# A pre-norm's squares summed in column groups beside a fourth output, and root's table loaded ahead of the post-norms

## The reference

```python
def rms_norm(x, g):
    y = x * lax.rsqrt(jnp.mean(x * x, axis=-1, keepdims=True) + 1e-6)
    return y * g

def squared_relu_mlp(h, w1, w2):            # w1 1024x4096, w2 4096x1024
    return jnp.square(jax.nn.relu(h @ w1)) @ w2

for layer in range(2):
    hn = rms_norm(h, mix_pre_g[layer])
    m = conformer_conv(hn, ...) if layer == 0 else mla_attention(hn, ...)
    h = h + rms_norm(m, mix_post_g[layer])
    f = squared_relu_mlp(rms_norm(h, ffn_pre_g[layer]), w_ff1[layer], w_ff2[layer])
    h = h + rms_norm(f, ffn_post_g[layer])
```

## Time and profile before

| | |
|---|---|
| median of 3 runs | 1212.76 us (1208.52 to 1216.09) |
| profiled execution | 1209.91 us, its span 1208.1 us |
| TensorE busy | 1160.0 us, 96% of the span |
| weight loads of TensorE (beside matmuls) | 993.7 us, 82% |
| VectorE, ScalarE, GpSimd busy | 848.7, 669.8, 213.5 us |
| mean granted clock of TensorE | 0.989 of full |
| HBM read | 205.09 MB, 172 GB/s |

### The profile page before, as it was taken

One profiled execution on the slowest core, in us unless ns is written; L12 is line 12 of the kernel. 1 busy time (PEld: TensorE's weight loads), 2 busy tenths in 40 slices (PEclk: granted clock), 3 DMA queues, 4 the chain that ended last, 5 costly groups with the idle time before them and its releaser, 6 DMA issues.

```text
span 1208.1 us, 26351 instructions
## 1 busy us (share of the span) xinstructions
PE 1160.0 (96%) x10538; PEld 993.7 (82%) x10538; DVE 848.7 (70%) x1390; ACT 669.8 (55%) x1024; POOL 213.5 (18%) x166
## 2 busy tenths in 40 slices
PE   8999999999899999999999999999999999999997
PEld 6888888888666888888877678888887777888886
DVE  5656876655864886555677468888777665888775
ACT  5435566433656566433565566665556656666542
POOL 0000000000002000000032433554231333355400
PEclk8999999999999999999999999999999999999999
DMA  7871355555251355555232334554465334455452
GB/s 292 275 243 65 118 222 208 209 207 195 86 209 71 139 209 210 209 189 190 108 106 106 139 140 156 217 215 152 175 242 196 109 116 179 162 209 211 142 196 78
DMA packets 22250, 208.37 MB, mean 172 GB/s; under 512 B 2464, under 2 KB 8992, under 8 KB 9120
## 3 DMA queue, kind: packets, MB, share of 16 engines
q1 hardware_dynamic: 22176, 207.32, 47.4%
HBM read 205.09 MB, written 2.23 MB: 172 GB/s over the span
## 4 chain that ended last, share of the span: by engine, by line
PE 54%; issue 17%; DVE 12%; POOL 6%; ACT 6%; DMA 4%; SPq 0%; POOLq 0%; DVEq 0%; ACTq 0%
PE ps L654 13%; PE ps L656 13%; PE ps L655 13%; POOL tmp L1941 5%; DVE w_lo L2013 4%; DMA staged<-weights 3%; ACT w_hi L1384 2%; POOL probs L1950 1%; PE ps L812 1%; PE ps L665 1%; PE ps L667 1%; PE ps L835 1%; PE ps L666 1%; PE ps L710 1%; PE ps L787 1%
## 5 line engine op out<-in xcount | busy, mean ns | idle before, releaser
L1384 ACT ACTIVATE w_hi<-staged 128x2048 f16<-128x2048 f32 (+1 forms) x192 | 356.2, 1870 | 196.9 <-PE ps L656 156.1
L2013 DVE SCALAR_TENSOR_TENSOR w_lo<-staged,w_hi 128x2048 f16<-128x2048 f32 (+1 forms) x192 | 429.3, 2249 | 44.1 <-ACT w_hi L1384 43.9
L654 PE MATMUL ps<-f_hi,w_hi 128*128 128x256 f16 x1596 | 435.1, 273 | 4.4 <-DVE w_lo L2013 2.1
L656 PE MATMUL ps<-f_hi,w_lo 128*128 128x256 f16 x1596 | 435.0, 273 | 0.0
L655 PE MATMUL ps<-f_lo,w_hi 128*128 128x256 f16 x1596 | 435.0, 273 | 0.0
L654 PE MATMUL ps<-x_hi,w_hi 128*128 128x256 f16 x928 | 253.8, 274 | 5.8 <-DVE x_lo L2043 2.9
L655 PE MATMUL ps<-x_lo,w_hi 128*128 128x256 f16 x928 | 253.4, 273 | 0.0
L656 PE MATMUL ps<-x_hi,w_lo 128*128 128x256 f16 x928 | 253.4, 273 | 0.0
L654 PEld LDWEIGHTS ps<-f_hi,w_hi 128*128 128x128 f16 x1596 | 156.1, 98 | 25.1 <-issue 3.4
L655 PEld LDWEIGHTS ps<-f_lo,w_hi 128*128 128x128 f16 x1596 | 156.2, 98 | 18.3
L656 PEld LDWEIGHTS ps<-f_hi,w_lo 128*128 128x128 f16 x1596 | 156.2, 98 | 18.1
(11 more groups left out here) (304 smaller groups left out, 1588.9 us busy)
## 6 DMA issues: line engine op xcount, KB each, us to landing
staged<-weights SPq DMA_DIRECT2D x82, 2048.0 KB, 8.1
staged<-weights SPq DMA_DIRECT2D x16, 1408.0 KB, 6.2
qT<-u_rows SPq DMA_DIRECT2D x16, 143.0 KB, 3.2
kT<-u_rows SPq DMA_DIRECT2D x16, 143.0 KB, 3.7
staged<-weights SPq DMA_DIRECT2D x2, 1024.0 KB, 8.3
u_rows<-probs SPq DMA_DIRECT2D x8, 144.0 KB, 4.6
cst<-constants SPq DMA_DIRECT2D x1, 1031.5 KB, 16.2
h<-x_turned SPq DMA_DIRECT2D x1, 1024.0 KB, 5.2
```

The costliest lines, as they stand in the source:

```text
L654: pe.matmul(out, wh, xh[:, c, :], start=(c == 0), stop=False)
L656: last = pe.matmul(out, wl, xh[:, c, :], start=False, stop=(c == kc - 1))
L1384: act.activation(w_hi[:, s, o:o + n], staged[:, s, o:o + n], ACT.Copy, scale=SW).then_inc(hi_split, 1)
L2013: dve.scalar_tensor_tensor(w_lo[:, s, o:o + n], staged[:, s, o:o + n], SW, w_hi[:, s, o:o + n], ALU.mult, ALU.subtract).then_inc(lo_split, 1)
```

## The change

Layers 0 and 1, norms `ffn_pre_0` and `ffn_pre_1` only (the loop ahead of the kv product keeps its three outputs and its own sums):

- The arrival loop has four outputs (`RING`) for three. It doesn't add a square per chunk. At chunk 5 and behind the loop `group_sums` sums four squares at once: four matmuls with a 32-column matrix of ones, each into its own 32 partitions of bank 7 (column groups), the second set accumulating on the first.
- ScalarE copies that bank to SBUF (`group_copied`); in output 4, ahead of chunk 4, TensorE sums the copy per token (each sum stands 32 times there, which the root's scale divides out); root and reciprocal run on 128x2; in output 5, ahead of chunk 1, TensorE spreads the scale; VectorE copies it to `LATE_SCALE` (`copy_late`), and only then drains.
- Outputs 4 and 5 of the first round go to banks 4 and 5 (`hidden_bank`), so they wait for no drain. Output 6 goes to bank 2 and waits for the third drain, output 7 to bank 3 and for the fourth.
- `root_next` is called ahead of the layer norm's squares, ahead of `square_last` of mix_post_0, behind the sines in `mlp(0)`, and ahead of the `wo` product's splits.

```diff
@@ -224,8 +224,14 @@
 ADDED = (*POSTS, "final")
 ADDED_AT = {_name: (DC - 1) * _i for _i, _name in enumerate(ADDED)}
 
-BY_TOKEN = ("mix_pre_0", "layer_norm", "mix_post_0", "ffn_post_0", "mix_post_1", "ffn_post_1", "attn_0",
+BY_TOKEN = ("mix_pre_0", "layer_norm", "mix_post_0", "ffn_pre_0", "ffn_post_0", "mix_post_1", "ffn_pre_1", "ffn_post_1", "attn_0",
             "g_ckv", "attn_1", "final")
+
+GROUPED = ("ffn_pre_0", "ffn_pre_1")
+GROUPS = 4
+
+
+LATE_COPIED = ("ffn_pre_0", "ffn_pre_1", "attn_0")
 
 SUM_BANK = {"layer_norm": 4, "attn_0": 4}
 COLUMN = {"g_ckv": 4}
...
@@ -550,6 +558,11 @@
         def even_bank(n):
 
             return n if n < 3 else (n - 3) % 2
+
+        def hidden_bank(i, n):
+
+
+            return n if isinstance(i, int) and i == 0 and n < RING + 2 else n % RING
 
         def wait_from(engine, semaphore, value):
 
@@ -734,6 +747,11 @@
                         return
                     pe.matmul(STAT, k("ones"), stat[:, 4, :], start=True, stop=True).then_inc(summed, 1)
                     return
+                if name in GROUPED:
+
+                    pe.wait_ge(group_copied, GROUPED.index(name) + 1)
+                    by_token(6, stat[:, 0, :], True, True).then_inc(summed, 1)
+                    return
                 if name in ADDED_AT:
 
                     pe.wait_ge(m_added, ADDED_AT[name] + n - 1)
@@ -764,6 +782,27 @@
                     last = pe.matmul(STAT, k("ones"), sq[:, c, :], start=(c == 0), stop=(c == DC - 1))
                 if c == DC - 1:
                     last.then_inc(summed, 1)
+
+            def group_sums(name, first):
+
+
+                if first == 0:
+                    pe.wait_ge(rooted, NORM_AT[name])
+                pe.wait_ge(squared, SQUARE_AT[name] + first + GROUPS)
+                n = P // GROUPS
+                for r in range(GROUPS):
+                    last = pe.matmul(ps[n * r:n * r + n, 7, 0:T], k("ones")[:, 0:n], sq[:, first + r, :], start=(first == 0),
+                                     stop=(first + GROUPS == DC))
+                if first + GROUPS == DC:
+                    last.then_inc(group_summed, 1)
+
+            def grouped(name):
+
+                def fresh(c):
+                    if c == GROUPS + 1:
+                        group_sums(name, 0)
+                    pe.wait_ge(x_lo_ready, SPLIT_AT[name] + c + 1)
+                return fresh
 
             def begun(name):
 
@@ -929,19 +968,30 @@
                 one, two = f"ff1_{layer}", f"ff2_{layer}"
                 u0 = FIRST[one]
 
-                def hidden_chunk(i, n):
+                def hidden_chunk(i, n, fresh=None):
 
                     s, j = n // 4, n % 4
                     if j % 2 == 0:
                         pe.wait_ge(lo_split, i * 4 + (2 * (u0 + s) + j // 2 + 1))
 
-                    wait_from(pe, drained[one], i * 8 + (n + 1 - RING))
-                    features(ps[:, n % RING, 0:T], (u0 + s) % 2, j * DC * P, DC, x_hi, x_lo).then_inc(product[one], 1)
-
-                together(one, 3, x_hi, x_lo, begun(f"ffn_pre_{layer}"))
-                add_square(f"ffn_pre_{layer}", DC - 1)
-                for n in range(3, 8):
-                    hidden_chunk(0, n)
+                    b = hidden_bank(i, n)
+                    if b < RING:
+                        wait_from(pe, drained[one], i * 8 + (n + 1 - RING))
+                    features(ps[:, b, 0:T], (u0 + s) % 2, j * DC * P, DC, x_hi, x_lo, fresh).then_inc(product[one], 1)
+
+                def norm_sums(n):
+
+                    def fresh(c):
+                        if (n, c) == (4, 4):
+                            sums(f"ffn_pre_{layer}")
+                        if (n, c) == (5, 1):
+                            spread_scale(f"ffn_pre_{layer}", inverted, NORM_AT[f"ffn_pre_{layer}"] + 1)
+                    return fresh
+
+                together(one, RING, x_hi, x_lo, grouped(f"ffn_pre_{layer}"))
+                group_sums(f"ffn_pre_{layer}", GROUPS)
+                for n in range(RING, 8):
+                    hidden_chunk(0, n, norm_sums(n))
                 with pe.Fori(1, dict(STREAM)[one] // 2) as i:
                     for n in range(8):
                         hidden_chunk(i, n)
@@ -1158,7 +1208,7 @@
                         dot(2 * n - 10)
                         dot(2 * n - 9)
                     if n == 6 and c == 1:
-                        pe.wait_ge(late_ready, 1)
+                        pe.wait_ge(late_ready, LATE_COPIED.index("attn_0") + 1)
                         sums("g_ckv")
                     if n == 7 and c == 1:
                         spread_scale("g_ckv", inverted, NORM_AT["g_ckv"] + 1)
@@ -1418,8 +1468,9 @@
                     dst, src = root_col[:, o:o + TT], ps[:, b:b + TT, 0]
                 else:
                     dst, src = stat[:, 0, :], STAT
+                copies = P // GROUPS if name in GROUPED else 1
                 act.activation(dst, src, ACT.Sqrt, bias=k("input_eps" if late else "rms_eps"),
-                               scale=(INV ** -2 if late else 1.0) / (P * NORM_CHUNKS[name])).then_inc(rooted, 1)
+                               scale=(INV ** -2 if late else 1.0) / (P * NORM_CHUNKS[name] * copies)).then_inc(rooted, 1)
 
             def square_last(name, norm, bank, scale, bias=0.0):
 
@@ -1540,6 +1591,7 @@
                     conv_out(j - CONV_LAG - 1)
             for c in range(DC - CONV_LAG - 1, DC):
                 conv_out(c)
+            root_next()
             for c in range(DC):
                 act.wait_ge(ln_centred, c + 1)
                 act.activation(sq[:, c, :], conv[:, c, :], ACT.Square).then_inc(ln_squared, 1)
@@ -1563,6 +1616,8 @@
                 one, two = f"ff1_{layer}", f"ff2_{layer}"
                 for c in range(DC):
                     begin(f"ffn_pre_{layer}", x_hi, h_ready[f"mix_{layer}"], 0, c)
+                act.wait_ge(group_summed, layer + 1)
+                act.activation(stat[:, 0, :], STAT, ACT.Copy).then_inc(group_copied, 1)
                 root(f"ffn_pre_{layer}")
                 u0 = FIRST[one]
 
@@ -2055,6 +2112,10 @@
                     return SPREAD_SCALE
                 dve.wait_ge(inverted, NORM_AT[name] + 1)
                 return stat[:, 1, :]
+
+            def copy_late(name):
+
+                dve.tensor_copy(LATE_SCALE, scale_there(name)).then_inc(late_ready, 1)
 
             def scale(name, src, gain, dst, lag=1, meanwhile=None):
 
@@ -2290,7 +2351,8 @@
 
                 split(2 * u0 + 2)
                 invert(f"ffn_pre_{layer}")
-                dve.wait_ge(inverted, NORM_AT[f"ffn_pre_{layer}"] + 1)
+                copy_late(f"ffn_pre_{layer}")
+                dve.wait_ge(late_ready, LATE_COPIED.index(f"ffn_pre_{layer}") + 1)
 
                 def hidden_low(i, n):
 
@@ -2305,7 +2367,7 @@
                     dve.wait_ge(product[one], i * 8 + (n + 1))
 
                     wait_from(dve, f_hi_ready[layer], i * 8 + (n - 1))
-                    dve.scalar_tensor_tensor(tmp[:, n % 2, :], ps[:, n % RING, 0:T], 0.0, LATE_SCALE, ALU.max,
+                    dve.scalar_tensor_tensor(tmp[:, n % 2, :], ps[:, hidden_bank(i, n), 0:T], 0.0, LATE_SCALE, ALU.max,
                                              ALU.mult).then_inc(drained[one], 1)
                     if n or not isinstance(i, int):
                         hidden_low(i, n - 1)
@@ -2500,7 +2562,7 @@
                 for i in E_SWAP.get(n, ()):
                     rope("even", i)
                 if n == 3:
-                    dve.tensor_copy(LATE_SCALE, SPREAD_SCALE).then_inc(late_ready, 1)
+                    copy_late("attn_0")
                 if n == 6:
                     forget_first()
                     weigh(0)
```

More of the change, by code:

```diff
@@ L417, in conformer_mla_fox_dsa_moba_kernel @@
         late_ready = sem("late_ready")
+        group_summed = sem("group_summed")
+        group_copied = sem("group_copied")
         part_product = sem("part_product")
@@ L1969, in decays @@
                         [P, T]), ALU.mult).then_inc(decay_rows, 1)
-            pool.wait_ge(late_ready, 1)
+            pool.wait_ge(late_ready, LATE_COPIED.index("attn_0") + 1)
             for n in (4, 5, 6, 7):
```

## The result

| | before | changed |
|---|---|---|
| median | 1209.82 us (19 runs, 1205.38 to 1216.15) | 1214.96 us (19 runs, 1208.98 to 1219.09) |
| ratio | | 1.0036, 95% interval 1.0021 to 1.0051 |
| span of the profiled execution | 1208.1 us | 1212.7 us |
| mean granted clock | 0.989 | 0.986 |

The ratio is estimated from all the runs of both kernels and is not that of the two medians, which differ by 5.1 us. By it the changed kernel is slower by 4.4 us (2.5 to 6.2), well inside the 1% that was called "same". The forecast of 1214.7 us looks closer than it is: it stood on the median 1212.76 of three runs, and 19 runs put before at 1209.82. What was forecast is a difference of +1.9 us; what was measured is +4.4. One execution of the kernel before in the experiments took 2407 us and is left out throughout.

The account below looks back on a forecast made before the run. It took TensorE, busy nearly the whole span, as the bound, so edits act only at the seams. Tables -1.1, loops +1.8 and clock +1.2 gave +1.9 us on the median 1212.76: 1214.7 us, range 1208 to 1219.

Parts of the forecast that it names:

- The table: Post-norms: early loads of root's table let the root start sooner, by 0.55, 0.62 and 0.08 us; counted as -1.1 us.
- The term of mix_post_0: Post-norm mix_post_0: root 0.55 us sooner, of which some 0.40 is left because more warm-up matmuls run at half clock.
- The rival by which the switch frees more than the load: Three post-norms: the table switch holds ScalarE up a load's length more, so 3 x 1.28 us more gained, 1210.9; chance 0.05.
- The four column groups: Arrival loops of layers 0 and 1: a set of four grouped square sums takes 0.68 us, bounds 0.44 and 1.74.
- The series rival: Arrival loops: the four groups run one after another, 1.74 us for 0.68 a set, +4.2 us, 1218.9; chance 0.12.
- their cover: Outputs 4 and 5: ScalarE's copy has 1.31 us, root and small reciprocal 2.01 us, before TensorE needs their results.
- The drain: Behind each loop: first drain 2.46 us later, TensorE waits 2.13 at output 6; output 7 +0.9 us, twice +1.8.
- The clock: Behind the output 6 waits: TensorE drops to half clock after one of two, +1.2 us, bounds 0 and +2.4.
- the drains don't bind: First hidden product, layers 0 and 1: only TensorE's own account counts, 1.71 us ahead per layer, -4.5, 1208.2; chance 0.12.

Follow-up runs that it names:

- tables_only: The kernel before with the four early table loads alone; ratio 0.9991 (0.9969 to 1.0014) to the kernel before.
- free_drains: The changed kernel with two half-unit weight splits moved out of the way of VectorE's drains; ratio 0.9977 (0.9952 to 1.0003) to the kernel before.
- early_spread: The changed kernel with per-token sum and spread moved forward to chunks 2 and 6 of output 4; ratio 1.0010 (0.9990 to 1.0030) to the kernel before.
- after_again: The changed kernel a second time, with no edit; ratio 1.0046 (1.0022 to 1.0069) to the kernel before.
- loop_only: The changed kernel without the four early table loads; ratio 1.0050 (1.0029 to 1.0071) to the kernel before.
- both_early: The changed kernel with both the splits of free_drains and the positions of early_spread; ratio 0.9965 (0.9944 to 0.9986) to the kernel before.

## Why the prediction was right or wrong

The direction, the class and the mechanism held; the difference was put too small, by two terms that were mis-sized: the table edit's in mix_post_0 and, above all, the clock's. That the total came within 0.3 us of the measured median is luck: the median it was added to stood 2.9 too high, the difference 2.5 too low.

- **The table.** Gains of 0.57, 0.61, 0.10 for 0.55, 0.62, 0.08, and none in the layer norm, whose root still waited 1.51 us for TensorE after the early load. The term of mix_post_0 was mis-sized: I let the half clock in its warm-up stay and took 0.40; it went, and layer 0's stretch shows 1.39. The rival by which the switch frees more than the load has no row for it: root 0.62 after the sum, as in the post-norm that never had a load.
- **The four column groups.** 136.60 - 135.83 = 0.77, less 0.11 for the fp16 matmul, is 0.66 us a set, for 0.68 taken from two groups of 64 columns. The series rival (1.74) is out. ScalarE's copy, the per-token sum and the spread fell inside their cover, as said.
- **The drain.** First drain 4.42 behind the loop's end for 4.45; wait at output 6 2.14 for 2.13; at output 7 0.38 for 0.47. I had TensorE start the loop late; here the chunk's arrival started it (0.54 idle at 129.12), since the warm-up ran at full clock, with no effect on what follows the loop. One loop costs 1.04 us (177.45 less 176.41 of tables_only) for the 0.9 forecast. free_drains shows that it is the queue behind the drain, early_spread that the drain's own start counts one for one.
- **The clock**, the term that failed in size. I counted one stretch behind two waits, at 1.2. In three profiles (changed, after_again, loop_only) five of the six waits of 2.14 us have half clock behind them. At the price of 1.28 that is 1.28 x 5 / 3 = 2.1 us a run, for 1.2. The fourteen seams of the other seven profiles, where the wait is 1.15 us or less or is filled, have none.
- **The sum again with measured terms**: tables -1.39 - 0.61 - 0.10 = -2.1, loops 2 x 1.04 = +2.1, clock +2.1: +2.1 us, just below the measured 2.5 to 6.2. About half of what lies above is clock too, by the clock on record with every run: 0.9851 on average over the changed kernel's 29 runs, 0.9878 over 69 runs of the kernel before. That is 36.1 and 29.4 us at half clock, 6.7 more (3.8 to 9.5). A us at half clock costs 0.38 us, by the slope of time against it within each kernel (182 runs), the same as 1.28 for a stretch of 3.41. By an estimate from these figures the clock's share of the difference is 2.5 us. The sum above holds 1.3 of it: 2.1, less the 0.8 by which the 1.39 of mix_post_0 exceeds its 0.57. With 1.2 more it comes to 3.3, inside the interval. In which places this further half clock lies is open. A candidate is mix_post_1's warm-up, 0.7 to 1.1 us of time where it comes: 6 of 10 profiles have it, with and without either edit, and I can't tie it to one. The other half clocks ahead of the seams (3.41, 6.83 or 10.24 us in the layer norm) change from one execution to the next as well.
- **The rival "the drains don't bind"**, 1208.2, was no outcome of this change, but its price was right: both_early builds it and stands 4.2 below before, for the 4.5 that it named.

## What to carry to other kernels

When a step is added to an in-order queue, ask what becomes late and what stands behind it on the engine that is waited for: here a scale 2 us later, with a weight split between the first two drains, turned an output gained in the loop (2.6 us) into a wait of nearly that length (2.1); moving that split into idle time some microseconds earlier gave it back. Prefer the place of a cross-engine step that it can just reach to one safely behind it. Price a wait of TensorE not only at its length: once it is as long as here, count what follows at half clock, or fill it with matmuls whose results nobody reads.

## What the runs showed that I had not expected

Half clock followed 2.14 us of waiting in five of six cases, and none of the waits of 1.15 us or less in the same place. The mean granted clock that each run records, profiled or not, shows such an effect over all runs, where a pair of profiles shows one execution each. Neither did I expect that mix_post_0's warm-up would have half clock in both profiles without the early table load and in none of the eight with it. The idle time ahead of the spread there fell from 1.20 us to 0.62. Whether that is the cause is not shown: ahead of mix_post_1's spread the same 0.62 us stand in profiles with half clock (changed) and without (both_early). TensorE's timelines, kernel before and changed kernel:

```profile
124.79 1.22 PE L718 MATMUL ps<-cst,root_col 128*128 128x128 f32 x4 [1.20 <-DVE root_col L2030]
```

```profile
126.14 0.71 PE L731 MATMUL ps<-cst,root_col 128*128 128x128 f32 x4 [0.62 <-DVE root_col L2087]
```

The spread itself takes 1.22 us in the one and 0.71 in the other: the first already runs at half clock, which begins at 124.49.

Filling a wait with fp32 matmuls on stale data cost nothing (177.45 and 177.45), and no half clock followed.
